# Four more norms in columns, five convolution taps and two product blocks moved to TensorE, and another order of row tiles

## Chip, cores and metric

The kernel runs on one core of one Trainium2 chip. The time is device microseconds of one execution, from the first instruction to the last with what lies around them; the lower the better. TensorE is called PE (its weight loads PEld), VectorE DVE, ScalarE ACT, GpSimd POOL, and SyncE SP, which here only issues transfers. SBUF is the memory on the core, and PSUM the eight banks (128 partitions of 512 fp32 numbers each) into which PE writes. A "wide" operation is one on 128x512 fp32.

## What is computed

Two transformer blocks on one sequence of 512 rows with 1024 channels, all in fp32. What the change touches, cut:

```python
def rmsnorm(x, g):
    y = x * rsqrt(mean(x * x, axis=-1, keepdims=True) + EPS)
    return y * g

def conformer_conv(hn, w_pw1, b_pw1, w_dw, b_dw, ln_g, ln_b, w_pw2, b_pw2):
    a, g = split(hn @ w_pw1 + b_pw1, 2)              # 1024 -> 2 x 1024
    u = a * sigmoid(g)
    u = causal_depthwise_conv(u, w_dw, width=31) + b_dw
    u = silu(layernorm(u, ln_g, ln_b))
    return u @ w_pw2 + b_pw2

# first block, layer 0: convolution; layer 1: 16 heads of forgetting attention
h = h + conformer_conv(rmsnorm(h, mix_norm[0]), ...)
h = h + square(relu(rmsnorm(h, ffn_norm) @ w1)) @ w2
h = h + sigmoid(rmsnorm(h, ple_norm) @ w_gate) * (p @ w_proj)
...
x = rmsnorm(h, final_norm)
# second block
hn = rms_norm(x, mix_norm_gain)
# hn @ w_in gives a linear recurrence, 8 heads of block attention and
# qx for 4 heads of 128 that attend to a memory of 256 rows
mk, mv = split(rms_norm(mem, mem_norm_gain) @ w_mem_kv)
p = softmax(qx @ mk.T * 128 ** -0.5); y_c = p @ mv    # per head
x = x + (sum of gated branches) @ w_out
x = x + (gelu(conv3(hn2 @ w_gate)) * (hn2 @ w_up)) @ w_down
return rms_norm(x, final_norm_gain)
```

## The kernel before

**Layout.** Activations lie transposed: a tile `h[:, k]` holds 128 channels of the 512 rows, and a 1024-wide tensor is eight tiles. A sum over channels is therefore a matmul with `inv_d`, a 128x128 matrix of 1/1024: squares of the eight tiles are added up by DVE in `acc_sq` (or by PE in PSUM), and one matmul with `inv_d` as the stationary operand gives the mean of squares in every partition, as a 128x512 row block. `norm` then adds EPS and takes the reciprocal on DVE (`var`), and ACT takes the root (`rstd`), all 512 wide. The other form stands in `col_stats`: four matmuls with one column of `inv_d` moving give the same mean as four columns of 128 rows, 128x4 in all.

**Products.** Each fp32 product is three matmuls in a faster fp32 form (`three`, L532 to L534): high times high, low times high, high times low. So each operand has a high and a low part. A block is 24 matmuls (8 channel tiles of the input, three each) into one bank, and it yields 128 output channels. Weights come from HBM in pieces of 1 MB, two parts of 128x1024 each. For every part ACT rounds the high half (L906, `next_w`), POOL subtracts it to get the low half (L435, `slab`), and PE's block waits for that. A ring of four parts lets the next one be made when a block of an older one has ended. The four banks `gp` take the products; the four banks `ms` take sums, scores and transposes.

**Order.** There is no scheduler: each engine runs its own program in the order in which it is written, and semaphores tie them. `next_w` and `slab` calls stand by hand between the other work of ACT and POOL.

**The stages, by the profile.** First norm and first product (to about 27 us); the convolution with the first product's other blocks (to 190); layer norm and second product (to about 250); feed-forward, gate, head attention, feed-forward, gate (to 1317); `qx`, memory attention (to 1362); gates, recurrence, block attention, feed-forward (to 2155); the last norm and the stores (to 2172).

**The convolution** goes over four pairs of channel tiles. Of the 31 taps of a tile, the first `POOL_TAPS[i]` are multiplied by ACT (`tap_products`) and added by POOL (`add_taps`, L458) in `pool_sum`; the others are one DVE step each (L1320), accumulating in a PSUM bank `ms`. `Weave` alternates the two tiles of a pair. `whole` adds the two sums. In between PE does the rest of the first product, two projections of p (`project`), the memory's statistics (`memory_stat`, `memory_turn`), and the products for memory keys and values (`memkv`), which need the memory's low half `m_lo` from POOL; then `mean` adds up the eight conv tiles for the layer norm.

**Layer norm.** DVE subtracts the mean from eight tiles (L1317), ACT squares each (L1043), PE adds the squares up in a bank (L671) with one wide matmul each, DVE does EPS and the reciprocal, ACT the root; then for each tile DVE multiplies, ACT applies silu (L1049) and rounds, DVE makes the low half, and `pw2` starts.

**Memory attention** (`attention`) takes 16 steps, 4 heads by 4 row tiles: scores (L842), maximum on DVE, exponential on ACT, two transposes on PE (L720), a copy, two matmuls with the values (L733) giving rows by channels, the division by the sum on DVE in `o_sb`, and after each head four more transposes (`O_`), then rounding. The first products behind it start when its last low half is there.

**Head attention** (`head_attention`) works on pairs of heads by row tile `qb` = 0, 1, 2, 3, whose width is (qb + 1) x 128 since attention is causal; steps are `S_` scores, `T_` transposes, `V_` values. It runs for 8 pairs in the first block and 4 in the second.

**Tail.** After the last blocks DVE adds (`add_h`, L1317), ACT squares, DVE adds the squares, one wide matmul, EPS, reciprocal, root, then eight wide DVE products into `h` and four stores.

## Time and profile before

| | |
|---|---|
| time, median of 3 runs | 2174.54 us (2173.0 to 2176.71) |
| profiled execution's own time | 2173.63 us |
| its span, first to last instruction | 2171.6 us |
| mean granted TensorE clock | 0.987 of full speed |
| PE, PEld busy | 2095.2 us, 1708.5 us |
| DVE, ACT, POOL busy | 1025.3, 799.8, 937.9 us |
| data read from HBM | 197.73 MB, 94 GB/s over the span |

The page gives for each engine its busy time as a share of the span, then for groups of instructions the mean length of one and the idle time just ahead of them with the instruction that ended it. The timeline gives single instructions or short runs of the same instruction, with the start in microseconds from the beginning of the span; a bracket at the end says how long the engine had been idle and on what it had waited. An fp32 matmul that isn't in the faster form shows as two records of one line. Matmuls are pipelined, so that one of 512 columns is listed with 0.39 us although the next starts 0.23 us after it.

### The profile page before, as it was taken

The page shows a single profiled execution, that of the slowest core. Times are in us where ns is not written, and L with a number is a line of the kernel's source. Part 1 is how long each engine was busy: PE and PEld are TensorE (multiplying, and loading weights), DVE is VectorE, ACT ScalarE, POOL GpSimd, SP SyncE. Part 2 cuts the span into 40 slices and gives each one's busy share as a digit, 9 for nine tenths or more (in the row PEclk, how much of TensorE's full clock was granted, in tenths as well). Part 3 has the DMA queues.
Part 4 walks back from the last instruction along what each step waited for, and adds up shares of the span by engine and source line. Part 5 has one row for each costly group of instructions (what it writes and reads, how often), then busy time and mean ns, then how long its engine had stood idle before and what let it go on. Part 6 is the DMA issues. An engine that isn't in the chain of part 4 may idle for free.

```text
span 2171.6 us, 26817 instructions
## 1 busy us (share of the span) xinstructions
PE 2095.2 (96%) x10024; PEld 1708.5 (79%) x10024; DVE 1025.3 (47%) x1584; ACT 799.8 (37%) x1213; POOL 937.9 (43%) x435
## 2 busy tenths in 40 slices
PE   7977999999999999999999998999999999999997
PEld 6765888888888876888888887778967888888885
DVE  7996432132355547442231356463354456254463
ACT  6645422222343248332222355252245343232231
POOL 5875454444444420354444442434442444444441
PEclk9988999999999999999999999999999999999998
DMA  4331242222222221332222221222211222322221
GB/s 189 112 131 59 80 154 97 97 97 97 97 97 99 98 78 41 116 117 97 97 97 97 97 88 49 83 97 97 89 67 53 84 97 97 104 90 103 91 97 58
DMA packets 32201, 205.28 MB, mean 95 GB/s; under 512 B 4448, under 2 KB 4576, under 8 KB 9072
## 3 DMA queue, kind: packets, MB, share of 16 engines
q1 hardware_dynamic: 31824, 199.87, 26.1%
q10 hardware_dynamic: 288, 4.19, 0.5%
q8 instruction: 59, 0.97, 0.2%
q14 instruction: 30, 0.25, 0.0%
HBM read 197.73 MB, written 6.32 MB: 94 GB/s over the span
## 4 chain that ended last, share of the span: by engine, by line
PE 58%; issue 24%; POOL 11%; DVE 5%; ACT 2%; DMA 0%; POOLq 0%; DVEq 0%; ACTq 0%
PE gp L532 18%; PE gp L533 18%; PE gp L534 18%; POOL w_lo L435 9%; DVE ms L1320 2%; POOL pool_sum L458 1%; DVE var L1346 0%; PE ms L671 0%; ACT w_hi L906 0%; PE ms L611 0%; DVE T L1317 0%; ACT T L1171 0%; PE ms L842 0%; DVE acc_sq L1317 0%; PE gp L808 0%
## 5 line engine op out<-in xcount | busy, mean ns | idle before, releaser
L435 POOL TENSOR_TENSOR w_lo<-raw,w_hi 128x1024 fp32r<-128x1024 f32 x350 | 847.6, 2424 | 1141.6 <-ACT w_hi L906 1124.1
L532 PE MATMUL gp<-a_hi,w_hi 128*128 128x512 f32 x1440 | 564.9, 392 | 12.4 <-DVE a_lo L1320 9.9
L906 ACT ACTIVATE w_hi<-raw 128x1024 fp32r<-128x1024 f32 x349 | 365.9, 1051 | 530.4 <-PE gp L534 525.6
L533 PE MATMUL gp<-a_lo,w_hi 128*128 128x512 f32 x1440 | 561.0, 390 | 0.0
L534 PE MATMUL gp<-a_hi,w_lo 128*128 128x512 f32 x1440 | 561.0, 390 | 0.0
L532 PE MATMUL gp<-b_hi,w_hi 128*128 128x512 f32 x1184 | 464.1, 392 | 8.6 <-DVE b_lo L1317 8.6
L533 PE MATMUL gp<-b_lo,w_hi 128*128 128x512 f32 (+1 forms) x1216 | 471.6, 388 | 0.0
L534 PE MATMUL gp<-b_hi,w_lo 128*128 128x512 f32 x1184 | 461.6, 390 | 0.0
L532 PEld LDWEIGHTS gp<-a_hi,w_hi 128*128 128x128 f32 x1440 | 271.0, 188 | 71.8 <-issue 13.1
L533 PEld LDWEIGHTS gp<-a_lo,w_hi 128*128 128x128 f32 x1440 | 271.1, 188 | 57.2 <-issue 1.5
L534 PEld LDWEIGHTS gp<-a_hi,w_lo 128*128 128x128 f32 x1440 | 270.7, 188 | 56.5
L1317 DVE TENSOR_TENSOR h<-gp,h 128x512 f32<-128x512 f32 x104 | 71.8, 692 | 429.9 <-PE gp L534 429.9
L532 PEld LDWEIGHTS gp<-b_hi,w_hi 128*128 128x128 f32 x1184 | 222.9, 188 | 56.9 <-issue 10.1
L533 PEld LDWEIGHTS gp<-b_lo,w_hi 128*128 128x128 f32 x1216 | 230.1, 189 | 47.3 <-issue 1.2
L534 PEld LDWEIGHTS gp<-b_hi,w_lo 128*128 128x128 f32 x1184 | 222.8, 188 | 46.4
L1317 DVE TENSOR_TENSOR T<-gp,rstd 128x512 f32<-128x512 f32 x136 | 93.8, 690 | 311.7 <-PE gp L534 308.7
L1320 DVE SCALAR_TENSOR_TENSOR ms<-u_pad,par,ms 128x512 f32<-128x512 f32 x178 | 120.5, 746 | 0.6
L915 ACT ACTIVATE sqb<-h 128x512 f32<-128x512 f32 x63 | 39.7, 632 | 146.7 <-DVE h L1317 127.4
L1320 DVE SCALAR_TENSOR_TENSOR T<-gpad,par,T 128x512 f32<-128x512 f32 x48 | 83.4, 1737 | 5.2 <-DVE T L1891 0.2
L458 POOL TENSOR_TENSOR pool_sum<-pool_sum,sqb 128x512 f32<-128x512 f32 x54 | 68.6, 1287 | 14.1 <-ACT sqb L975 13.9
L1064 ACT ACTIVATE b_hi<-U 128x512 fp32r<-128x512 f32 x32 | 20.3, 633 | 121.3 <-DVE U L1320 121.3
L1064 ACT ACTIVATE a_hi<-U 128x512 fp32r<-128x512 f32 x32 | 20.3, 633 | 120.4 <-DVE U L1320 120.4
(289 smaller groups left out, 1906.4 us busy)
## 6 DMA issues: line engine op xcount, KB each, us to landing
raw<-w_hbm SPq DMA_DIRECT2D x176, 1024.0 KB, 4.9
proj_scratch<-kT ACTq DMA_DIRECT2D x2, 2048.0 KB, 6.6
fbias<-negc_scratch SPq DMA_DIRECT2D x16, 256.0 KB, 3.4
h<-x_hbm SPq DMA_DIRECT2D x4, 512.0 KB, 7.1
u_pad<-proj_scratch SPq DMA_DIRECT2D x1, 2048.0 KB, 9.7
big<-proj_scratch SPq DMA_DIRECT2D x1, 2048.0 KB, 8.7
out_hbm<-h SPq DMA_DIRECT2D x4, 512.0 KB, 2.7
mem_raw<-mem_hbm SPq DMA_DIRECT2D x1, 1024.0 KB, 12.1
```

What stands on the lines that cost most here:

```text
L435: g.tensor_tensor(at(w_lo), src, f32(at(w_hi)), ALU.subtract).then_inc(w_lo_done, 1)
L458: g.tensor_tensor(pool_sum[:, s], pool_sum[:, s], sqb[:, s], ALU.add).then_inc(pool_conv, 1)
L532: pe.matmul(o, wh, xh, start=start, stop=False)
L533: pe.matmul(o, wh, xl, start=False, stop=False)
L534: return pe.matmul(o, wl, xh, start=False, stop=stop)
L906: act.activation(at(w_hi), src, ACT.Copy).then_inc(w_hi_done, 1)
L915: act.activation(dst, h[:, c], ACT.Square).then_inc(sq_done, 1)
L1064: act.activation(H_[0][:, k], U[:, k % 2], ACT.Copy).then_inc(hi_done, 1)
L1317: return v.tensor_tensor(o, a, b, op)
L1320: return v.scalar_tensor_tensor(o, a, s, b, op0, op1)
```

## The change

**1. Norms in columns.** For the first norm, the layer norm, the norm ahead of the second block (two chained norms, `gate[1]` and `fin`) and the last one, the wide mean, EPS, reciprocal and root are replaced. `columns` gives the mean as 128x4 in PSUM, `inverse_column` (DVE) does EPS and reciprocal on 128x4, `root_of` (ACT) the root. `diagonal` puts each of the four columns on the diagonal of a 128x128 matrix (two on DVE, two on ACT), and `spread` multiplies them with `inv_d`, which fills a bank with the root as rows in every partition. DVE copies it to `rstd`, or reads it in the bank. In the first norm the columns are made inside the first product, which now takes two blocks side by side (`first_blocks`, hook at the eighth channel tile).

**2. Convolution.** Pair 3 has five taps on POOL instead of eight, five on PE (`pe_taps`: a matmul of the shifted tile with the tap's weights on a diagonal, made by ACT in `diagonals`) and 21 on DVE instead of 23. PE's taps come first in the bank; DVE waits for them (`pe_tap_done`) and adds to them. PE's taps stand between the first and second half of the second projection, which is split likewise on ACT. The memory turn and the means use bank `ms[0]`, and the turn now waits for the end of the third pair's first sum. On POOL the weight part 23 moves from ahead of `m_lo` to behind it. One of four value tiles (of `memkv`) moves behind the layer norm's `spread`.

**3. Weight parts at the layer norm.** On ACT the part 28 is rounded after the last square, 29 after the first silu, 30 after the last silu and the two last value copies.

**4. Memory attention.** The values are stationary, so that a step's output comes with channels on partitions and the four turning transposes and `o_sb` go; probabilities are divided by their sum before they are transposed (`weighted`). Two blocks of the next product (`gxg`) stand inside: behind the second scores, and behind the last.

**5. Row tiles.** Both head attentions take the row tiles in the order 0, 3, 1, 2.

**6. Tail.** The last tile's squares go to the columns without DVE's addition. ACT and POOL scale tiles 0 and 1, DVE the other six; five stores in another order.

```diff
-POOL_TAPS = (9, 7, 7, 8)
+POOL_TAPS = (9, 7, 7, 5)
+PE_TAPS = (0, 0, 0, 5)
...
-STAT_TAP, COLUMN_TAP, KEYS_TAP = 3, 2, 15
+STAT_TAP, COLUMN_TAP, KEYS_TAP = 3, 4, 13
...
+ROW_TILE = (0, 3, 1, 2)
...
+
+        def pe_diag(s, n):
+
+            return T[:, 2 * s, n * P:n * P + P] if n < 4 else U[:, 1, s * P:s * P + P]
...
-            slab(Pos(23))
             g.wait_ge(m_hi, 1)
             g.tensor_tensor(M[1], mem_raw[:], f32(M[0]), ALU.subtract).then_inc(m_lo, 1)
-            add_taps(3, {3: [24], 5: [25], 7: [26], 9: [27], 12: [28], 13: [29]})
-            slabs(pw2["slab"] + 2, gq["slab"] + AHEAD)
+            add_taps(3, {1: [23], 3: [24], 4: [25], 5: [26], 7: [27]})
...
+            g.wait_ge(rows_copied, 1)
+            for k in range(2):
+                g.wait_ge(out_scaled, k + 1)
+                g.tensor_tensor(h[:, k], h[:, k], rstd[:], ALU.mult).then_inc(out_first, 1)
```

PE:

```diff
+            def columns(src, at, start=True, stop=True):
+
+                for t in range(QB):
+                    m = pe.matmul(at[:, t:t + 1], src[:, t * P:t * P + P], inv_d[:, 0:1], start=start, stop=stop, skip_group_check=True)
+                return m
...
+            def spread(n, diag, bank):
+
+                pe.wait_ge(diag_v, 2 * n + 2)
+                pe.wait_ge(diag_a, 2 * n + 2)
+                for t in range(QB):
+                    m = pe.matmul(bank[:, t * P:t * P + P], inv_d[:], diag[:, t * P:t * P + P], start=True, stop=True,
+                                  skip_group_check=True)
+                m.then_inc(row_done, 1)
+
+            def x_columns():
+                pe.wait_ge(acc_done, x0["acc"] + 7)
+                columns(acc_sq, ms[:, 1]).then_inc(stat_x, 1)
...
+            def pe_taps(s):
+                pe.wait_ge(u_done, 7 + s)
+                pe.wait_ge(diag_done, PE_TAPS[3] * (s + 1))
+                for n in range(PE_TAPS[3]):
+                    m = pe.matmul(ms[:, 1 + s, :], pe_diag(s, n), u_of(6 + s, TAPS - PE_TAPS[3] + n), start=(n == 0),
+                                  stop=(n == PE_TAPS[3] - 1))
+                m.then_inc(pe_tap_done, 1)
+            first_blocks(pw1[0], A, x0["split"], hook=x_columns, hook_k=7)
+            spread(0, x_diag, ms[:, 3])
+            pair(0, 2)
...
-            project(0)
+            project(0, 0)
+            project(0, 1)
             pair(3)
-            project(1)
+            project(1, 0)
+            pe_taps(0)
+            pe_taps(1)
+            project(1, 1)
             memory_turn()
...
-            for s in range(2):
-                slab_xs(Pos(memkv["slab"] + 4 + 2 * s), Pos(memkv["blk"] + 4 + 2 * s), M, 2)
...
+            slab_xs(Pos(memkv["slab"] + 4), Pos(memkv["blk"] + 4), M, 2)
+            slab_xs(Pos(memkv["slab"] + 6), Pos(memkv["blk"] + 6), M, 1)
             mean(6)
             mean(7).then_inc(mean_done, 1)
             for k in range(8):
                 pe.wait_ge(csq_done, k + 1)
-                pe.matmul(ms[:, 2, :], inv_d[:], sqb[:, k % 2], start=(k == 0), stop=(k == 7)).then_inc(cvar_done, 1)
+                if k == 0:
+                    clear_columns(ms[:, 3])
+                columns(sqb[:, k % 2], ms[:, 3], False, k == 7).then_inc(cvar_done, 1)
+            spread(1, ln_diag, ms[:, 1])
+            slab_xs(Pos(memkv["slab"] + 6), Pos(memkv["blk"] + 6), M, 1, 1)
             first_blocks(pw2, B, ln["split"])
...
+                def T_(i):
+                    pe.wait_ge(weighted, at["weighted"] + i + 1)
...
+                    for kb in range(2):
+                        m = pe.matmul(gp[:, 2 + j % 2, t * P:t * P + P], mv[:, kb, j * P:j * P + P],
+                                      probT[i % 4][:, kb * P:kb * P + P], start=(kb == 0), stop=(kb == 1), skip_group_check=True)
+                    m.then_inc(pv_done, 1)
+
+                for i in range(N + 4):
+                    if i < N:
+                        S_(i)
+                    if i in (1, N):
+                        slab_ws(Pos(gxg["slab"] + i // N), Pos(gxg["blk"] + i // N), A)
+                    if 3 <= i < N + 3:
+                        T_(i - 3)
+                    if i >= 4:
+                        V_(i - 4)
+            memory_attention()
...
-            gemm(gxg, A)
+            for c in range(2):
+                pe.wait_ge(lo_done, xat["split"] + 3 + c)
+                rest_of(gxg, A, 2 + c, 3 + c)
+            rest_of(gxg, A, 4, 8)
...
+            pe.wait_ge(acc_done, f["acc"] + 6)
+            columns(acc_sq, ms[:, 1], False, False)
+            pe.wait_ge(sq_done, f["sq"] + 8)
+            columns(sqb[:, 1], ms[:, 1], False, True).then_inc(stat_x, 1)
+            spread(4, end_diag, ms[:, 0])
+            spread(4, end_diag, ms[:, 2])
```

ACT and DVE (`columns`, `diagonal` and the attention steps that only follow the same pattern are left out):

```diff
-                         {5: lambda: sigmoid(3, 0), 10: lambda: sigmoid(3, 1), 12: lambda: projected(1, 0)})
-            projected(1, 1)
-            next_w(Pos(23 - AHEAD))
-            tap_products(3, {4: [24], 6: [25], 8: [26], 10: [27], 13: [28], 14: [29]}, {})
-            for s in range(2):
-                memory_values(s)
-            next_of(memkv, 7)
+                         {1: lambda: diagonals(0), 3: lambda: diagonals(1), 5: lambda: sigmoid(3, 0), 10: lambda: sigmoid(3, 1),
+                          12: lambda: projected(1, 0, 4)})
+            tap_products(3, {4: [23], 5: [24], 6: [25], 7: [26], 9: [27]}, {1: lambda: projected(1, 4, 5), 3: lambda: projected(1, 5, 8)})
...
                     act.wait_ge(cvar_done, k - 1)
...
+            next_w(Pos(28 - AHEAD))
+            act.wait_ge(c_inv, 2)
+            root_of(1, colv[:])
+            diagonal(1, ln_diag)
             for k in range(8):
                 act.wait_ge(normed, k + 1)
                 if k >= 2:
@@ -1049,6 +1115,10 @@
                 act.activation(U[:, k % 2], big[:, k], ACT.Silu, bias=col("ln_b", k), scale=col("ln_g", k)).then_inc(silu_done, 1)
...
                 act.activation(b_hi[:, k], U[:, k % 2], ACT.Copy).then_inc(hi_done, 1)
+                if k == 0:
+                    next_w(Pos(29 - AHEAD))
+            memory_values(1)
...
 
@@ -1128,51 +1198,18 @@
...
+                def H_(j):
+                    act.wait_ge(pv_done, at["pv"] + 4 * (j + 1))
+                    act.activation(b_hi[:, 4 + j], gp[:, 2 + j % 2], ACT.Copy).then_inc(hi_done, 1)
...
+            def inverse_column(n, src):
+
+                v.tensor_scalar(colv[:], src, EPS, 2.0 ** -20, ALU.add, ALU.mult).then_inc(c_eps, 1)
+                v.wait_ge(c_eps, n + 1)
+                v.reciprocal(colv[:], colv[:]).then_inc(c_inv, 1)
+
+            def diagonal(n, diag):
+
+                v.wait_ge(root_done, n + 1)
+                for t in range(2):
+                    v.tensor_scalar(diag[:, t * P:t * P + P], ident[:], root[:, n % 2, t:t + 1], None, ALU.mult).then_inc(diag_v, 1)
+            v.wait_ge(stat_x, 1)
...
+                src, sum_ = u_of(c, t), conv_bank(i, s)
+                if n == 0 and i == 3:
+                    v.wait_ge(pe_tap_done, s + 1)
...
+            inverse_column(1, ms[:, 3, 0:QB])
+            diagonal(1, ln_diag)
+            v.wait_ge(row_done, 2)
             for k in range(9):
                 if k < 8:
...
+            v.wait_ge(row_done, 5)
+            for k in range(2, 8):
+                stt(h[:, k], h[:, k], col("final2", k), ms[:, 0], ALU.mult, ALU.mult).then_inc(out_ready, 1)
```

**Where instructions stand.** PE at the end of the second projection, in a row before: `p_hi`, `p_lo` are the projection, `inv_d,U` is the memory turn, `b_lo` the first product on the memory.

```order
L532 MATMUL gp<-p_hi,w_hi 128x512
L533 MATMUL gp<-p_lo,w_hi 128x512
L534 MATMUL gp<-p_hi,w_lo 128x512
L634 MATMUL ms<-inv_d,U 128x1 [waits u_done,mrstd_done]
L634 MATMUL ms<-inv_d,U 128x1
L532 MATMUL gp<-b_lo,w_hi 128x256 [waits evacuated0,w_lo_done,mem_lo]
```

And now:

```order
L555 MATMUL gp<-p_hi,w_hi 128x512
L556 MATMUL gp<-p_lo,w_hi 128x512
L557 MATMUL gp<-p_hi,w_lo 128x512
L695 MATMUL ms<-u_pad,T 128x512 [waits tap_diagonal,u_done]
L695 MATMUL ms<-u_pad,T 128x512 x3
L695 MATMUL ms<-u_pad,U 128x512
L695 MATMUL ms<-u_pad,T 128x512 [waits tap_diagonal,u_done]
L695 MATMUL ms<-u_pad,T 128x512 x3
L695 MATMUL ms<-u_pad,U 128x512
L555 MATMUL gp<-p_hi,w_hi 128x512 [waits evacuated0,w_lo_done,p_lo_done]
```

The ten taps stand ahead of the projection's second half, and the turn comes behind that half.

ACT at the layer norm before (`sqb<-u_pad` are the squares, `rstd` the root, `U` the silu, `b_hi` its rounding):

```order
L1043 ACTIVATE sqb<-u_pad 128x512 [waits centred,proj_stored1]
L1043 ACTIVATE sqb<-u_pad 128x512 [waits centred]
L1043 ACTIVATE sqb<-u_pad 128x512 [waits cvar_done,centred] x6
L925 ACT_TABLE_LOAD
L925 ACTIVATE rstd<-var 128x512 [waits var_done]
L1049 ACT_TABLE_LOAD
L1049 ACTIVATE U<-u_pad,par 128x512 [waits normed]
L1051 ACTIVATE b_hi<-U 128x512 [waits silu_done]
```

And now:

```order
L1106 ACTIVATE sqb<-u_pad 128x512 [waits centred,proj_stored1]
L1106 ACTIVATE sqb<-u_pad 128x512 [waits centred]
L1106 ACTIVATE sqb<-u_pad 128x512 [waits cvar_done,centred] x6
L955 ACTIVATE w_hi<-raw 128x1024 [waits blk_done,raw_ready0]
L1001 ACT_TABLE_LOAD
L1001 ACTIVATE root<-colv 128x4 [waits column_inv]
L998 ACTIVATE T<-ident,root 128x128 [waits root]
L998 ACTIVATE T<-ident,root 128x128
L1115 ACT_TABLE_LOAD
L1115 ACTIVATE U<-u_pad,par 128x512 [waits normed]
L1117 ACTIVATE b_hi<-U 128x512 [waits silu_done]
L955 ACTIVATE w_hi<-raw 128x1024 [waits blk_done,raw_ready0]
```

A weight part comes between the last square and the root, and another behind the first silu; the root is four columns wide.

PE at the start of memory attention before (`mkv,qx` are scores, `ident,T` transposes, `mkv,U` values):

```order
L842 MATMUL ms<-mkv,qx 128x256 [waits evacuated2,evacuated3,evacuated1,evacuated0]
L842 MATMUL ms<-mkv,qx 128x256 [waits exped] x2
L720 MATMUL ms<-ident,T 128x128 [waits exped]
L720 MATMUL ms<-ident,T 128x128
L842 MATMUL ms<-mkv,qx 128x256 [waits exped]
L720 MATMUL ms<-ident,T 128x128 [waits exped]
L720 MATMUL ms<-ident,T 128x128
L733 MATMUL gp<-mkv,U 128x128 [waits pt_copied]
L733 MATMUL gp<-mkv,U 128x128
L842 MATMUL ms<-mkv,qx 128x256 [waits exped]
```

And now, first the start, then what follows the block of 24:

```order
L683 MATMUL ms<-T,inv_d 128x128 [waits diag_act,diag_dve]
L683 MATMUL ms<-T,inv_d 128x128 x3
L852 MATMUL ms<-mkv,qx 128x256 [waits evacuated0]
L852 MATMUL ms<-mkv,qx 128x256
L555 MATMUL gp<-a_hi,w_hi 128x512 [waits evacuated0,w_lo_done]
```

```order
L852 MATMUL ms<-mkv,qx 128x256 [waits exped] x2
L859 MATMUL ms<-ident,T 128x128 [waits weighted]
L859 MATMUL ms<-ident,T 128x128
L852 MATMUL ms<-mkv,qx 128x256 [waits exped,evacuated1]
L859 MATMUL ms<-ident,T 128x128 [waits weighted]
L859 MATMUL ms<-ident,T 128x128
L870 MATMUL gp<-U,mkv 128x128 [waits pt_copied,evacuated2]
L870 MATMUL gp<-U,mkv 128x128
```

A whole block stands behind the second scores, the transposes wait for weighted probabilities, and the values are now the stationary operand (`gp<-U,mkv`).

## Rows read from the trace of the kernel before

**Rows 1.** Page, part 1: busy us (share of span) xinstructions, by engine.

```profile
PE 2095.2 (96%) x10024; PEld 1708.5 (79%) x10024; DVE 1025.3 (47%) x1584; ACT 799.8 (37%) x1213; POOL 937.9 (43%) x435
```

**Rows 2.** Timeline, tail: start us, length us, engine, line, operation [idle before <-releaser].

```profile
2149.61 0.69 DVE L1317 TENSOR_TENSOR h<-gp,h 128x512 f32<-128x512 f32 x1 [4.15 <-PE gp L534]
...
2155.05 0.69 DVE L1317 TENSOR_TENSOR h<-gp,h 128x512 f32<-128x512 f32 x1 [4.15 <-PE gp L534]
...
2163.12 5.39 DVE L1320 SCALAR_TENSOR_TENSOR h<-h,par,rstd 128x512 f32<-128x512 f32 x8 [0.70 <-ACT rstd L925]
```

**Rows 3.** Timeline of the start, PE and DVE.

```profile
19.80 2.07 PE L611 MATMUL ms<-acc_sq,inv_d 128*128 128x512 f32 x2 [2.75 <-DVE acc_sq L1317]
...
29.54 0.75 DVE L1320 SCALAR_TENSOR_TENSOR u_pad<-ms,par,T 128x512 f32<-128x512 f32 x1 [0.79 <-ACT T L960]
```

**Rows 4.** Timeline of the convolution, DVE, with one row of PE.

```profile
96.11 11.94 DVE L1320 SCALAR_TENSOR_TENSOR ms<-u_pad,par,ms 128x512 f32<-128x512 f32 x18
...
145.66 1.39 DVE L1408 TENSOR_SCALAR ms<-u_pad,par 128x512 f32<-128x512 f32 x2
...
155.04 0.58 PE L532 MATMUL gp<-b_lo,w_hi 128*128 128x256 f32 x1 [8.84 <-POOL b_lo L476]
...
187.68 0.69 DVE L1317 TENSOR_TENSOR u_pad<-ms,pool_sum 128x512 f32<-128x512 f32 x1 [2.90 <-POOL pool_sum L458]
189.59 4.87 DVE L1317 TENSOR_TENSOR u_pad<-u_pad,ms 128x512 f32<-128x512 f32 x8 [1.22 <-PE ms L661]
```

**Rows 5.** Timeline of the layer norm and the product behind it.

```profile
200.90 3.35 DVE L1346 RECIPROCAL var<-var 128x512 f32<-128x512 f32 x1
...
204.94 1.28 ACT L1049 ACT_TABLE_LOAD   x1
...
206.23 0.81 ACT L1049 ACTIVATE U<-u_pad,par 128x512 f32<-128x512 f32 x1
...
208.69 0.77 PE L532 MATMUL gp<-b_hi,w_hi 128*128 128x512 f32 x1 [8.55 <-DVE b_lo L1317]
...
222.34 0.39 PE L532 MATMUL gp<-b_hi,w_hi 128*128 128x512 f32 x1
```

**Rows 6.** Timeline of memory attention and the sums before it, PE.

```profile
1317.34 1.02 PE L830 MATMUL ms<-acc_fin,inv_d 128*128 128x512 f32 x2
1318.20 0.95 PE L833 MATMUL ms<-inv_d,acc_sq 128*128 128x1 f32 x8
1319.01 1.03 PE L833 MATMUL ms<-inv_d,acc_fin 128*128 128x1 f32 x8
...
1331.43 1.10 PE L842 MATMUL ms<-mkv,qx 128*128 128x256 f32 x4 [1.73 <-DVE qx L1320]
...
1343.18 0.60 PE L842 MATMUL ms<-mkv,qx 128*128 128x256 f32 x2
...
1344.28 0.60 PE L842 MATMUL ms<-mkv,qx 128*128 128x256 f32 x2
...
1349.46 0.60 PE L842 MATMUL ms<-mkv,qx 128*128 128x256 f32 x2
...
1361.87 0.49 PE L532 MATMUL gp<-a_hi,w_hi 128*128 128x512 f32 x1 [1.69 <-DVE b_lo L1317]
```

**Rows 7.** Head attention: busy us in one period; timeline of a widest tile.

```profile
829.40:838.70 9.30, 9.11 (x88) 5.68 (x86) 7.11 (x30) 7.76 (x26) 0.00 (x0) 1.00 0.17 56
...
859.16 0.69 DVE L1676 CUSTOM_DVE_ANT_0 T<-gp,fbias 128x512 f32<-128x512 f32 x1 [1.41 <-PE ms L797]
```

**Rows 8.** Page, part 5: groups, busy us, mean ns | idle before, releaser.

```profile
L435 POOL TENSOR_TENSOR w_lo<-raw,w_hi 128x1024 fp32r<-128x1024 f32 x350 | 847.6, 2424 | 1141.6 <-ACT w_hi L906 1124.1
...
L906 ACT ACTIVATE w_hi<-raw 128x1024 fp32r<-128x1024 f32 x349 | 365.9, 1051 | 530.4 <-PE gp L534 525.6
...
L458 POOL TENSOR_TENSOR pool_sum<-pool_sum,sqb 128x512 f32<-128x512 f32 x54 | 68.6, 1287 | 14.1 <-ACT sqb L975 13.9
```

**Rows 9.** Waits of PE, whole span: us in total, times, longest us.

```profile
PE ms L797 <- DVE T L1687: 3.9, 5, 1.1
```

448 lines of the change are left out of this document (211 added, 237 removed).

## The prediction

> **What bounds the kernel now.** I read the busy line of the page first: the tensor engine (PE) is busy 96% of the span, the next engine half of it [rows 1]. So the time is PE's program plus its gaps, and a change pays where it takes products away from PE or closes a gap in which PE waits. Next comes PE's timeline, for every place where two products start further apart than their length. From about 223 us on one block of a 1024x1024 product (24 matmuls) ends every 5.44 us, as the two additions at the end show (2149.61 and 2155.05) [rows 2]; vector engine (DVE), scalar engine (ACT) and GpSimd (POOL) only have to keep up. Five places are left. (1) The first norm: PE waits 2.75 us up to 19.80 for the sum of squares [rows 3]. (2) The convolution: PE waits 8.84 us up to 155.04, while DVE works tap by tap [rows 4]. (3) The layer norm behind it: 8.55 us of waiting up to 208.69 [rows 5]. (4) Memory attention, 1331.43 to 1361.87, with small products and waits [rows 6]. (5) The tail, from the last addition at 2155.05 [rows 2] to the end of the span, 2171.6. The two head attentions are nearly full: in one period of four row tiles PE is busy 9.11 of 9.30 us [rows 7].
>
> **Prices.** A full fp32 matmul of 512 columns holds PE 0.85 us (1317.34 to 1318.20); four column matmuls take 0.81 (1318.20 to the next group, 1319.01) [rows 6]. So a norm in columns gives PE nothing; it shortens DVE's part, where one reciprocal over 128x512 takes 3.35 us [rows 5]. Spreading the root back is four matmuls of 128 columns, together one of 512: 0.85. A tap costs DVE 11.94/18 = 0.66 us [rows 4], PE 0.85, and on POOL 1.29 for the addition. A weight part costs ACT 1.05 and POOL 2.42 [rows 8]. Diagonal making is nowhere in the trace: 128x128 on DVE or ACT lies between 0.2 (the 4-wide steps, with their hand-over) and 0.4 (half of a 128x256 step); I take 0.3.
>
> **The start.** The first two blocks now run side by side: 42 matmuls before the statistic instead of 24, so the sum of squares (there before 19.80) no longer holds PE. Columns, two 4-wide DVE steps, a 4-wide root, the diagonals, a spread and a copy give DVE the row at about 24.9 instead of 26.7, and block 2 of the pair is there at once: the first gated input, at 29.54 now [rows 3], comes at about 27. PE is 4 us ahead, but DVE is the longer chain, so 2.5 us count.
>
> **The convolution.** Pairs 0 to 2 are unchanged and DVE has no gap in them, so pair 3 begins at 145.66 - 2.5 = 143.2 [rows 4]. It has 42 taps on DVE instead of 46: 27.8, with the memory column and keys 1.6 and the two sums 1.3, done at 173.9. Today it is ready too, but POOL is not: DVE waits 2.90 us at 187.68 for POOL's sum, after another wait before it [rows 4]. POOL loses six of its 14 additions (7.7 us) and the weight part ahead of the memory's low half: that half (2048 columns, so a little under twice a part's 2.42: 4.5 us) is done at about 146, then five parts and eight additions, 22.4, with some 2 of waiting: 170.6, hidden. PE gets ten taps, 8.5 us, right behind the first half of the second projection at about 133.5, where it waits now. With the second half of the projection (5.4) and about 1.4 for products at 1.2 GHz it reaches the memory's products at 149, finds the low half ready (the 8.84 us go), and needs 11.5 + 5.1 + 8.7 + 1.7 for memory keys, six means, three value tiles and the last two means: 176.3. DVE's first centring, at 189.59 now, comes then: 13.3 earlier, and PE is late by 2 us over DVE. The two are nearly even.
>
> **The layer norm.** The squares and their sums stay paced by a PE step per tile (0.81 for 0.85): 10.3 us, to 186.7. Now 200.90 + 3.35 is a reciprocal, and the root follows it. In the change DVE has its 4-wide result at 187.2, but ACT comes from the last square (185.5) through a weight part (1.05) and the table load (1.28 [rows 5]) and takes the root at 187.8. Diagonals, spread and product: 190.4. PE fills the gap with the fourth value tile (2.9). But new waits arise: weight part 29 is rounded only after the first silu, so POOL has its low part at 190.4 + 0.81 + 0.63 + 1.05 + 2.42 = 195.4 (0.81 is the silu [rows 5]; 0.63, the rounding behind it, I put between that and half of a part's 1.05), and part 30 only after all eight silus at 1.42 each: ACT is there at 204.7, POOL at 207.2. The third block of this product starts at 222.34 now [rows 5], so **15.1 us are gained** here, though the norm alone looks like more. Between 208.69 and 222.34 PE did 48 matmuls in 13.65 us, where 10.9 are needed at 2.4 GHz; that this loss at 1.2 GHz goes or stays changes nothing, since part 30 is later anyway. Ends: 10 (PE's tiles behind DVE at 1.2 GHz, 3 to 5 us) and 18 (POOL and ACT without any waiting).
>
> The trace has the silu start at 206.23, right behind the load that began at 204.94 and took 1.28 [rows 5]. The Trainium skill (ScalarE: Activation LUTs, "What ACT_TABLE_LOAD costs") adds a drain of about 1.38 us to each switch of table, 2.66 in all. With it the root would come 1.4 us later here and at the tail, and the sum would be 2.8 us worse, 2141.6. The trace shows no such drain, so the row decides.
>
> **Memory attention.** The sums before it cost PE the same as today: two 0.85 matmuls go, two 0.85 spreads come. DVE's two long reciprocals go, so the queries are there as PE ends their blocks, and scores start at 1329.4 instead of 1331.43. A step of scores, transposes and values is 1.10 us (1343.18 to 1344.28); with the turning of each head's output and its waits four steps take 6.28 now (1343.18 to 1349.46) [rows 6]. The turning goes. 16 steps at 1.10 and two product blocks at 5.44 are 28.5; the first block covers the first softmax. I add 2.0, because ACT has about 1.15 per step. The third block starts at 1359.9, against 1361.87 + 10.88 = 1372.75: **12.8 gained**. Ends: 7.3 (steps stay at 1.57) and 14.8. POOL's three clears before weight part 3 take 1 us and still end in time.
>
> **The tail.** After 2155.05: addition 0.7, square 0.65, columns 0.85, two steps 0.45, root 0.25 (its table load, 1.28 long, starts with the square's end and is just over), diagonals 0.6, spread 0.9, six products at 0.67: 2163.6. The other two tiles go over ACT and POOL (0.85 + 0.65 + 2 x 1.29 from 2159.5) and also end at 2163.6. Today the products end at 2163.12 + 5.39 and the span 3.1 us later [rows 2], so the end lies at 2166.7 to 2168: **4.4 gained**, 3 to 5.
>
> **The row tiles.** The order 0, 3, 1, 2 gives each step of PE a more even load. There is little to win: 0.19 idle in 9.30, twelve such periods, and the ends of both stages; PE waits 3.9 us in all for DVE's weighted rows [rows 9]. **2.5 gained**, from 8 gained to 2 lost.
>
> The sum is 15.1 + 12.8 + 4.4 + 2.5 = 34.8 off the profiled execution's 2173.6: 2138.8. The median shown, 2174.5, lies 0.9 above, so I say **2139**.
>
> **Rivals.**
> - The convolution gains less: PE's taps at 1.2 GHz (1.7 instead of 0.85 each) hold up the projection, ACT waits there in front of its products for POOL, and all comes 6 us later. For it: PE slows after each of today's waits; against: nothing waits ahead of the taps. 2145.
> - Memory attention keeps today's pace, and the second block hides nothing: 7 of the 12.8 stay. For it: ACT has as much to do per step as PE. 2146.
> - Everything hides and the row order takes up the small gaps between instructions: 5 from it, 3 more from the convolution. 2131.
> - The new row order starves PE: the widest tile comes second, and its two maxima (0.69 each [rows 7]), its two exponentials, about as long each, and the weighting, 3.7 us, stand open in each of 12 periods: 44 us, and 2185, slower than now. It decides from 3.1 us a period. Against it: between the wide tile's scores and its transposes PE has about 6 us of other tiles.
>
> **Chances.** Forecast (2134 to 2142) 0.58, convolution weak 0.16, attention weak 0.10, everything hides 0.12, starved 0.04. About 0.2% is what a measurement can tell here. The range holds all but the last and the edges of the others: 2130 to 2149. All but the starved case are faster: 0.95, and 0.02 within 0.2%, 0.03 slower.
>
> **What would show it.** Right: the first centring near 176; the third block of the product behind the layer norm at 207, with PE waiting for POOL's low weight part; the third block behind memory attention 12 to 13 us closer to the query blocks; a tail of 12 us after the last addition; head attention periods of 9.1 to 9.3. Wrong: a wait of DVE for PE's taps at the start of pair 3, a gap between POOL's additions beyond 174, or waits of PE for weighted rows in every period. The forecast would fail by the place of ACT's weight parts above all, as several of them wait in front of work on the path.

## The result, and the profile after

| | before | changed |
|---|---|---|
| median | 2173.77 us (4 runs, 2172.93 to 2176.71) | 2150.98 us (4 runs, 2148.33 to 2151.75) |
| span of the profiled execution | 2171.6 | 2148.5 |
| granted clock, mean | 0.987 | 0.991 |

The ratio of the runs is 0.9888, 95% interval 0.9875 to 0.9900; the medians lie 22.8 us apart (0.9895). I had forecast 34.8 us, and 2139 with a range to 2149: the direction was right, the gain half again as large as what came, and the time lies 2 us above the range. The changed kernel timed once more later gave 2150.36 (0.9878, 0.9859 to 0.9898).

The busy line of the page, against [rows 1]:

```profile
PE 2103.2 (98%) x10144; PEld 1723.6 (80%) x10144; DVE 1010.2 (47%) x1584; ACT 802.7 (37%) x1230; POOL 932.8 (43%) x432
```

PE has 8 us more work and DVE 15 us less; the idle part of PE shrank from 76.4 to 45.3 us. Laid side by side, the two traces give the gain stage by stage, each by the time at which the same instruction begins:

| stage | from, to | before | changed | gain | predicted |
|---|---|---|---|---|---|
| start, convolution, layer norm | 0 to the third block behind it | 222.34 | 212.45 | 9.9 | 15.1 |
| first head attention | first scores to the product behind | 788.91 to 866.55 | 779.11 to 856.12 | 0.6 | } 2.5 |
| second head attention | last product to next product | 1609.51 to 1652.51 | 1588.14 to 1630.26 | 0.9 | } |
| memory attention with its norm | statistics to the third block | 1316.49 to 1372.89 | 1306.04 to 1351.43 | 11.0 | 12.8 |
| tail | last addition to the end | 2155.05 to 2171.6 | 2132.78 to 2148.5 | 0.8 | 4.4 |
| sum | | | | 23.2 | 34.8 |

(The spans differ by 23.1. The forecast had put the third block behind memory attention at 1372.75, two blocks of 5.44 behind 1361.87 of [rows 6]; in the trace of before it begins at 1372.89.) So two rows hold 8.8 of the 11.7 us that are missing: the first, nearly all of it in the layer norm, and the tail. In the second trace of the changed kernel, of an execution of 2152.99 us, the third block behind the layer norm comes at 215.66 and the first row would read 6.7. First the part that came out as forecast. Timeline of DVE and PE in the start and the convolution of the changed kernel (columns as in [rows 2]); it answers to [rows 3] and [rows 4]:

```profile
21.97 0.95 PE L671 MATMUL ms<-inv_d,acc_sq 128*128 128x1 f32 x8
...
25.75 0.69 DVE L1550 COPY rstd<-ms 128x512 f32<-128x512 f32 x1 [1.59 <-PE ms L683]
28.55 0.75 DVE L1393 SCALAR_TENSOR_TENSOR u_pad<-ms,par,T 128x512 f32<-128x512 f32 x1 [0.80 <-ACT T L1020]
...
135.14 3.59 PE L695 MATMUL ms<-u_pad,T 128*128 128x512 f32 x8
...
144.49 6.70 DVE L1393 SCALAR_TENSOR_TENSOR ms<-u_pad,par,ms 128x512 f32<-128x512 f32 x10
...
173.52 1.33 DVE L1390 TENSOR_TENSOR u_pad<-ms,pool_sum 128x512 f32<-128x512 f32 x2
176.97 1.28 DVE L1390 TENSOR_TENSOR u_pad<-u_pad,ms 128x512 f32<-128x512 f32 x2 [2.12 <-PE ms L719]
```

The first gated input comes at 28.55 (29.54 before), so the start gives 1.0 and not 2.5: the copy of the row runs from 25.75 to 26.44 and ends 1.5 later than I had it. Pair 3 runs from 144.49 to 174.85 without a gap. PE's five taps for the first tile end at 139.6, 4.9 us before DVE adds to them; those for the second end at 143.88, 1.3 us before DVE's step at 145.14. So DVE waits for neither, but the second margin is thin: at the low clock (1.7 us a tap instead of 0.85) it would be gone. The first centring comes at 176.97, where I had 176.3; before it came at 189.59. Up to here 12.6 of the forecast 13.3 us are there. POOL is no longer waited for.

Then the layer norm, ACT, DVE, POOL and PE, against [rows 5]:

```profile
178.68 10.63 PE L671 MATMUL ms<-inv_d,sqb 128*128 128x1 f32 x64
182.54 0.63 ACT L1106 ACTIVATE sqb<-u_pad 128x512 f32<-128x512 f32 x1 [0.26 <-PE ms L671]
184.29 0.63 ACT L1106 ACTIVATE sqb<-u_pad 128x512 f32<-128x512 f32 x1 [1.12 <-PE ms L671]
185.99 0.63 ACT L1106 ACTIVATE sqb<-u_pad 128x512 f32<-128x512 f32 x1 [1.07 <-PE ms L671]
...
189.35 0.16 DVE L1454 TENSOR_SCALAR colv<-ms 128x4 f32<-128x4 f32 x1 [7.50 <-PE ms L671]
...
189.76 0.21 ACT L1001 ACTIVATE root<-colv 128x4 f32<-128x4 f32 x1 [0.89 <-DVE colv L1456]
...
190.84 2.05 PE L683 MATMUL ms<-T,inv_d 128*128 128x128 f32 x8 [1.53 <-ACT T L998]
...
192.92 1.28 DVE L1390 TENSOR_TENSOR u_pad<-u_pad,ms 128x512 f32<-128x512 f32 x2 [2.44 <-PE ms L683]
...
193.65 0.82 ACT L1115 ACTIVATE U<-u_pad,par 128x512 f32<-128x512 f32 x1 [1.65 <-DVE u_pad L1390]
...
196.15 2.37 POOL L455 TENSOR_TENSOR w_lo<-raw,w_hi 128x1024 fp32r<-128x1024 f32 x1 [6.16 <-ACT w_hi L955]
...
197.19 1.88 DVE L1390 TENSOR_TENSOR b_lo<-U,b_hi 128x512 fp32r<-128x512 f32 x1 [2.98 <-PE gp L557]
...
199.35 0.75 PE L555 MATMUL gp<-b_hi,w_hi 128*128 128x512 f32 x1 [2.20 <-DVE b_lo L1390]
...
212.45 0.50 PE L555 MATMUL gp<-b_hi,w_hi 128*128 128x512 f32 x1 [0.34 <-POOL w_lo L455]
```

And the same stretch in windows (us from to; length, busy us and instructions of PE, PEld, DVE, ACT, POOL; the third number from the end is the granted clock):

```profile
178.70:182.00 3.30, 3.30 (x32) 3.30 (x31) 3.14 (x6) 1.84 (x4) 0.00 (x0) 1.00 0.00 0
182.00:189.30 7.30, 7.30 (x36) 7.22 (x36) 0.00 (x0) 4.40 (x6) 1.65 (x1) 0.52 0.00 0
189.30:192.90 3.60, 2.07 (x11) 2.09 (x11) 0.82 (x4) 2.19 (x4) 0.69 (x1) 0.50 0.00 0
192.90:199.30 6.40, 4.25 (x24) 4.04 (x23) 3.40 (x4) 3.74 (x5) 2.37 (x1) 0.76 0.00 0
```

The reader is to see four things. ACT's squares come 0.9 apart to 182.54 and then 1.7 apart, since each waits for a column group of PE. The granted clock in the same stretch falls from 1.00 to 0.52 and 0.50, that is from 2.4 to 1.2 GHz, while PE is busy 7.30 of 7.30 us. And DVE waits 2.98 us, up to 197.19, for PE: for the fourth value tile, whose input lies where DVE wants to write the first low half (2.1 us of it once the rounded half that it also needs is there, at 195.12). And this low half then takes 1.88 us, while POOL makes weight part 29 (196.15 to 198.52); before, with POOL idle, it took 0.69:

```profile
207.74 0.69 DVE L1317 TENSOR_TENSOR b_lo<-U,b_hi 128x512 fp32r<-128x512 f32 x1 [1.49 <-ACT b_hi L1051]
```

The third block waits for POOL's part 30 last, as I had said, for 0.34 us. But that part comes at 212.40 and not at 207.2, since ACT rounds it behind the silus, and they began late and were held up by DVE.

### The profile page after: what moved, and what is told of

It reads as the page before. It is cut to its first block, busy times and chain, and to the rows that moved or that the text cites. A ratio compares the mean times of both kernels' runs of the same rounds, so it can differ in the third digit from the quotient of the medians.

```text
span 2148.5 us, 27006 instructions
## 1 busy us (share of the span) xinstructions
PE 2103.2 (98%) x10144; PEld 1723.6 (80%) x10144; DVE 1010.2 (47%) x1584; ACT 802.7 (37%) x1230; POOL 932.8 (43%) x432
## 3 DMA queue, kind: packets, MB, share of 16 engines
q1 hardware_dynamic: 31968, 199.87, 26.4%
## 4 chain that ended last, share of the span: by engine, by line
issue 40%; PE 36%; POOL 18%; DVE 3%; ACT 1%; POOLq 0%; DMA 0%; DVEq 0%; ACTq 0%
POOL w_lo L455 16%; PE gp L555 12%; PE gp L557 11%; PE gp L556 11%; DVE ms L1393 2%; POOL pool_sum L478 1%; ACT sqb L1035 0%; PE gp L870 0%; PE gp L810 0%; DMA raw<-w_hbm 0%; PE gp L788 0%; ACT w_hi L955 0%; POOL b_lo L495 0%; POOLq L454 0%; PE ms L799 0%
## 5 line engine op out<-in xcount | busy, mean ns | idle before, releaser
L478 POOL TENSOR_TENSOR pool_sum<-pool_sum,sqb 128x512 f32<-128x512 f32 x48 | 61.2, 1288 | 12.8 <-ACT sqb L1035 12.7
```

The costliest lines, as they stand in the source:

```text
L478: g.tensor_tensor(pool_sum[:, s], pool_sum[:, s], sqb[:, s], ALU.add).then_inc(pool_conv, 1)
```

## Experiments

All are built on the changed kernel. In brackets behind a time stand the ratio to the kernel before, run beside it, and its 95% interval. The diffs are cut. In the tables "first product" is the first matmul of the second projection of the convolution, and "next stage" the first matmul of the feed-forward layer with a low part; between them PE does eight blocks. These come from one trace each and place a difference to 0.1 us; the times of whole runs of one kernel lie 1 to 5 us apart.

### e1: the value tile between the column groups

```diff
                 columns(sqb[:, k % 2], ms[:, 3], False, k == 7).then_inc(cvar_done, 1)
...
+                s, at = sp_.slot(RING, k // 4), k % 4 * 256
+                m = three(gp[:, vb, 0:256], M[0][:, k, P:2 * P], M[1][:, k, P:2 * P], w_hi[:, s, at:at + 256], w_lo[:, s, at:at + 256],
+                          k == 0, k == 7)
+            m.then_inc(blk_done, 1)
             spread(1, ln_diag, ms[:, 1])
-            slab_xs(Pos(memkv["slab"] + 6), Pos(memkv["blk"] + 6), M, 1, 1)
```

> The changed kernel, with the 24 matmuls of the fourth value tile set in threes behind each of the eight column groups of the layer norm instead of behind the spread. In the changed kernel the eight groups run from 178.68 to 189.3 with the granted clock at 1.00, then 0.55 and 0.50, the spread behind them at 0.50, the first low half waits 2.98 us for the value tile, and the third block starts at 212.45. Clock theory: half of the loss is that PE runs these small matmuls at 1.2 GHz. With more work between them it stays at 2.4: the groups take 9.6 us, the spread 0.85 instead of 1.7, the first product comes at about 194 instead of 199.35, and the third block at about 207, 5 us earlier. Rival, the clock costs nothing because squares set the pace: only the wait for the tile goes, the groups still take 10.6 or more, the third block comes at 209.5, 3 us earlier.

2152.11 us (0.9896, 0.9879 to 0.9912), not faster at all. The windows of this run (columns as above), from the first group on:

```profile
178.00:182.00 4.00, 4.00 (x36) 4.00 (x36) 3.19 (x6) 1.88 (x4) 0.00 (x0) 0.96 0.00 0
182.00:193.00 11.00, 11.00 (x54) 11.00 (x53) 0.00 (x0) 4.39 (x6) 2.35 (x1) 0.50 0.00 0
```

PE had waited 1.50 us ahead of the first group, as in all traces with eight groups, and had no gap in the 15 us behind it. The clock fell at 181.67 all the same and stayed at 0.50, and then each group with its three products took 2.35 us. Both expectations fail: three products of 256 columns between the groups don't keep the clock up, and the groups get dearer with them. The first product came at 199.92, the next stage at 247.79.

### e2: weight parts earlier

```diff
             memory_values(0)
+            next_w(Pos(28 - AHEAD))
+            next_w(Pos(29 - AHEAD))
...
-            next_w(Pos(28 - AHEAD))
             act.wait_ge(c_inv, 2)
...
-                if k == 0:
-                    next_w(Pos(29 - AHEAD))
+                if k == 1:
+                    next_w(Pos(30 - AHEAD))
             memory_values(1)
-            next_w(Pos(30 - AHEAD))
```

> The changed kernel, with ACT rounding weight parts 28 and 29 ahead of the squares, where it idles 4.90 us, and part 30 behind the second silu instead of behind the last. The prediction held that the third block is set by part 30: then it comes 3 us or more earlier than 212.45. Clock theory: PE reaches the third block only at 212.1 anyway, since its first product starts late, at 199.35; the gain is 0.5 us at most, and the root is not earlier either.

2148.21 us (0.9874, 0.9858 to 0.9890). In this trace PE never waits for POOL's part. First product at 200.82 and next stage at 246.06: 45.2 us, against 46.1 in both traces of the changed kernel. By the traces the parts are worth about 0.9 us and not 3. PE's wait for POOL's part at the third block was 0.3 us in the first trace of the changed kernel and 1.7 in the second, and 1.7 to 1.8 in e3, e4, e8 and e11, which share its code here (0.3 in e7), always behind a late first product; the median is 2.2 to 2.8 us below the two of the changed kernel, within the scatter of its runs. So the parts end last, but taking their wait away brings only 0.9: the two limits lie close together, and what made both late stands ahead of the first product.

### e3: row tiles in the old order

```diff
-ROW_TILE = (0, 3, 1, 2)
+ROW_TILE = (0, 1, 2, 3)
```

> The changed kernel with the row tiles of both head attentions in the order 0, 1, 2, 3 as before. The prediction gave the new order 2.5 us. The two traces show 0.6 us less from one product to the next over the first head attention and 0.9 over the second: then this run is 1.5 us slower than the changed kernel, and the first attention takes as long as before. Rival, the order does nothing and these 1.5 us come from drift elsewhere: no difference.

2152.21 us (0.9893, 0.9877 to 0.9910). Over the second head attention the next product starts 43.00 us after the last one, exactly as before the change, and 42.12 in the new order. The first takes 79.2 against 77.0. Its windows, in e3, then in the changed kernel, then before:

```profile
781.40:860.60 79.20, 75.46 (x674) 46.86 (x674) 57.88 (x232) 63.27 (x201) 2.35 (x1) 0.98 0.13 41
```
```profile
779.10:856.10 77.00, 73.46 (x674) 46.02 (x674) 58.12 (x232) 64.23 (x201) 2.36 (x1) 1.00 0.14 42
```
```profile
788.90:866.50 77.60, 73.95 (x674) 46.03 (x674) 57.83 (x232) 63.18 (x201) 2.36 (x1) 1.00 0.13 42
```

In e3 the clock had 0.98 here, since it was down from 790.39 to 793.80, which costs about 1.7 us; before the change the old order took 77.6. PE's waits in this stretch are the same 3.3 to 3.7 us in sum in all three. The new order is worth 0.6 + 0.9 = 1.5 us (forecast 2.5), and the starved case did not occur.

### e4: the two product blocks behind memory attention

```diff
                     if i < N:
                         S_(i)
-                    if i in (1, N):
-                        slab_ws(Pos(gxg["slab"] + i // N), Pos(gxg["blk"] + i // N), A)
...
+            rest_of(gxg, A, 0, 2)
             for c in range(2):
                 pe.wait_ge(lo_done, xat["split"] + 3 + c)
...
-                    if i in (9, 13):
-                        next_of(gxg, i // 4 - 2)
+                    if i == 9:
+                        next_of(gxg, 0)
                 H_(3)
             memory_attention()
+            next_of(gxg, 1)
```

> The changed kernel with the two product blocks of memory attention moved from inside it to behind it, and ACT's second weight part there with them. If the blocks cover the first softmax and the last weighting, they are worth what PE waits there: before the change about 2.6 us between the first scores and the first transposes and about 1.5 at the end, so 4 to 5.5 us slower than the changed kernel. If ACT sets the pace of the 16 steps, the blocks hide nothing: under 1 us.

2149.48 us (0.9883, 0.9866 to 0.9899). From the first scores to the third block: 1321.46 to 1354.32, 32.9 us, against 32.2 (1319.22 to 1351.43). So the blocks inside are worth 0.7 us, or a little more, since ACT's second weight part also left the steps here. The rows of e4 show what the first softmax costs without a block to cover it:

```profile
1321.46 1.03 PE L852 MATMUL ms<-mkv,qx 128*128 128x256 f32 x4
1323.34 1.16 PE L852 MATMUL ms<-mkv,qx 128*128 128x256 f32 x4 [0.85 <-ACT T L1255]
...
1325.24 0.67 PE L852 MATMUL ms<-mkv,qx 128*128 128x256 f32 x2 [0.53 <-ACT T L1255]
```

PE waits 0.85 and 0.53 us. In the kernel before it had waited 1.87 us for the first exponential. There the same stretch, first scores to third block, took 41.5 us (1331.43 to 1372.89). So with no block inside 8.6 of the 9.3 us are there: the gain of this stretch is the turning and the shorter chain, not the cover (up to 1.7 us of it is the clock, which before was down from 1333.94 to 1337.35).

### e8: ACT's weight parts at the product blocks

```diff
-                    if i in (9, 13):
-                        next_of(gxg, i // 4 - 2)
+                    if i in (1, N):
+                        next_of(gxg, i // N)
```

> The changed kernel with ACT's two weight parts inside memory attention moved from the 9th and 13th step to the two places where PE runs a product block and ACT idles. In the changed kernel PE waits or slips 1.1 to 1.2 us behind each of the two parts. If these are the 1.9 us by which memory attention fell short of the prediction: 2 us faster from the first scores to the third block (32.2 us in the changed kernel). If the steps are bound elsewhere: no difference.

2147.67 us (0.9876, 0.9860 to 0.9893). First scores to third block: 1322.45 to 1354.21, 31.8 us, 0.4 less (this trace is of an execution of 2152.36 us; the other three took 2147.5 to 2147.7). In the changed kernel most steps start 1.10 us apart, but the values of two steps come 2.26 behind the ones before them. In e8 they come 1.79 behind, and 0.77 us of waiting for ACT's copy came in the last group. So the parts are a quarter of the missing 1.8 us, and the two slips stay, with 0.69 each. They stand where a head ends, in the changed kernel (first slip) at:

```profile
1334.06 0.69 DVE L1390 TENSOR_TENSOR b_lo<-gp,b_hi 128x512 fp32r<-128x512 f32 x1 [0.70 <-ACT b_hi L1267]
...
1335.12 0.47 ACT L1256 ACTIVATE T<-ms,nmax 128x256 f32<-128x256 f32 x1 [0.82 <-DVE nmax L1812]
```

DVE waits for ACT's rounding of the head and makes its low half, and only then the next maximum, for which ACT waits. With 28.5 us for 16 steps and two blocks, as forecast, 3.7 us come on top, where I had added 2.0; PE stands idle in 2.0 of them.

### e5: wide matmuls behind each column group

```diff
                 columns(sqb[:, k % 2], ms[:, 3], False, k == 7).then_inc(cvar_done, 1)
+                fill(2, ms[:, 2])
```

(`fill(n, bank)` is n matmuls of 512 columns into that bank.)

> The changed kernel with two additional matmuls of 512 columns (0.23 us each, into a bank nobody reads) behind each of the eight column groups of the layer norm. In all traces with the column form the granted clock falls to 0.50 between 178.5 and 182 and stays there to 196, even in the run in which the value tile's products filled every gap between the groups. In the kernel before, with 512-column sums, the same stretch had 0.86. If what lowers the clock is the one-column matmuls and wide ones hold it: the clock stays at 1.00, the groups come 1.27 us apart (10.2 in all, against 10.7 to 13.3), the spread takes 0.85, the first product comes at about 196.5 instead of 199.9 to 202, and the run is 2 to 4 us faster. If the clock falls in this place whatever PE does: groups of 2.6 us, 10 us slower.

2157.65 us (0.9923, 0.9906 to 0.9939), 7 us slower than the changed kernel. The trace is of the fastest of its four executions, 2153.80 us.

```profile
177.00:180.00 3.00, 3.00 (x25) 2.83 (x24) 3.00 (x6) 1.39 (x3) 0.00 (x0) 1.00 0.00 0
180.00:194.20 14.20, 14.20 (x60) 13.23 (x58) 0.22 (x1) 4.92 (x7) 2.36 (x1) 0.50 0.00 0
```

The clock fell at about 180, earlier than in the changed kernel, and stayed down for the 14 us of the sums; the groups came 2.56 us apart. Two matmuls of 512 columns in each step did not hold it.

### e6 and e10: squares added by DVE, one column group

```diff
+            slab_xs(Pos(memkv["slab"] + 6), Pos(memkv["blk"] + 6), M, 1, 1)
             for k in range(8):
-                pe.wait_ge(csq_done, k + 1)
-                if k == 0:
-                    clear_columns(ms[:, 3])
-                columns(sqb[:, k % 2], ms[:, 3], False, k == 7).then_inc(cvar_done, 1)
-            spread(1, ln_diag, ms[:, 1])
-            slab_xs(Pos(memkv["slab"] + 6), Pos(memkv["blk"] + 6), M, 1, 1)
+            for _ in range(20):
+                pe.matmul(ms[:, 2], a_hi[:, 0, 0:P], a_hi[:, 1], start=True, stop=True, skip_group_check=True)
+            pe.wait_ge(cvar_done, 7)
+            columns(acc_sq, ms[:, 3]).then_inc(cvar_done, 1)
+            spread(1, ln_diag, ms[:, 1])
```

(This is e6; e10 leaves the 20 matmuls out. The diff shows PE's part; ACT squares the first tile into `acc_sq`, and on DVE an addition into it stands behind the centrings.)

> The changed kernel with the eight squares of the layer norm added up by DVE (7 additions of 0.68, as before the first product), one column group at the end instead of eight, the fourth value tile run by PE in the meantime, and 20 wide matmuls into an unread bank behind it. Clock theory: this takes the one-column work at the low clock off the path. Sum on DVE: 8 centrings of 0.61 and 7 additions, 10 us, done at 187.5; columns and root at 189, rows at 190.5, and the first low half waits for no value tile: first product at 193.5 to 195, third block at 206 to 208, 5 to 7 us faster than the changed kernel. If ACT's later parts set the third block after all, 3 us or less.

> As e6_dve_sums (squares added by DVE, one column group, value tile in the meantime), without the 20 additional matmuls. In e6_dve_sums the clock fell to 0.50 at about 186.5 all the same, as the one column group began, so the additional matmuls bought nothing: the same time as e6_dve_sums within 1 us. If they did hold the clock for a while: the spread and the group take the same 3.4 us, but the clock is down at 182, and it may be back earlier or later, 1 us either way.

e6: 2145.83 us (0.9867, 0.9851 to 0.9884). e10: 2146.69 us (0.9861, 0.9845 to 0.9878). The first product comes at 195.25 and 195.85, the next stage at 243.58 and 244.02. So taking seven of eight column groups off the path gives 4 to 5 us, and the 20 matmuls nothing that can be told: in e6 the clock was up to 186.49 and down when the one group ran, in e10 it was down from 183.24 on, while PE waited 6.70 us. The group takes 1.87 us and the spread 2.05 in both.

### e9: the layer norm in the wide form

```diff
-                if k == 0:
-                    clear_columns(ms[:, 3])
-                columns(sqb[:, k % 2], ms[:, 3], False, k == 7).then_inc(cvar_done, 1)
-            spread(1, ln_diag, ms[:, 1])
+                pe.matmul(ms[:, 3, :], inv_d[:], sqb[:, k % 2], start=(k == 0), stop=(k == 7)).then_inc(cvar_done, 1)
...
-            inverse_column(1, ms[:, 3, 0:QB])
-            diagonal(1, ln_diag)
-            v.wait_ge(row_done, 2)
+            v.tensor_scalar(var[:], ms[:, 3], EPS, None, ALU.add).then_inc(eps_done, 1)
+            finish_var(ln)
+            v.wait_ge(rstd_done, ln["norm"] + 1)
...
-                    tt(big[:, k], big[:, k], ms[:, 1], ALU.mult).then_inc(normed, 1)
+                    tt(big[:, k], big[:, k], rstd[:], ALU.mult).then_inc(normed, 1)
```

> The changed kernel with the layer norm alone put back to the wide form (eight sums of 512 columns, EPS and reciprocal on 128x512, root as rows), everything else as changed, the fourth value tile behind the sums. In the kernel before, the wide form took 13.9 us from the first square's sum (191.05) to the first normalised tile (204.95); in the changed kernel and its variants the column form took 14.5 (178.44 to 192.92) where the clock fell late and 17.1 (177.97 to 195.12) where it fell early. If the columns at 1.2 GHz eat what the short reciprocal saves, the wide form here takes 14 us again, PE has the value tile done in the meantime, the first product comes at about 195.5 and the third block at 208 to 209: 3 to 5 us faster than the changed kernel. If the columns pay for themselves as the prediction had it (5 us less on DVE): 2 us or more slower.

2146.08 us (2145.77 to 2147.02; 0.9861, 0.9844 to 0.9877). Its four runs lie below all eight of the changed kernel (2148.24 to 2152.99), and so do all 16 of the kernels without the eight groups (e6, e9, e10 and e12: 2142.89 to 2148.08); the intervals of the ratios of e9 and the changed kernel overlap. Timeline of PE, DVE and ACT, and the windows:

```profile
177.58 7.70 PE L730 MATMUL ms<-sqb,inv_d 128*128 128x512 f32 x16 [1.50 <-ACT sqb L1103]
...
186.04 3.35 DVE L1414 RECIPROCAL var<-var 128x512 f32<-128x512 f32 x1
...
190.08 1.28 ACT L1110 ACT_TABLE_LOAD   x1
190.09 1.29 DVE L1385 TENSOR_TENSOR u_pad<-u_pad,rstd 128x512 f32<-128x512 f32 x2 [0.69 <-ACT rstd L971]
191.37 0.81 ACT L1110 ACTIVATE U<-u_pad,par 128x512 f32<-128x512 f32 x1
...
193.90 0.77 PE L555 MATMUL gp<-b_hi,w_hi 128*128 128x512 f32 x1 [5.75 <-DVE b_lo L1385]
...
196.52 0.80 PE L555 MATMUL gp<-b_hi,w_hi 128*128 128x512 f32 x1 [1.00 <-POOL w_lo L455]
...
177.60:185.30 7.70, 7.70 (x18) 2.81 (x19) 3.39 (x6) 5.42 (x9) 0.17 (x1) 1.00 0.00 0
185.30:190.10 4.80, 2.85 (x24) 2.65 (x23) 4.05 (x3) 1.70 (x3) 2.23 (x1) 1.00 0.00 0
```

With sums of 512 columns the clock stays at 1.00 to beyond 190. They take 7.7 us for the eight tiles, the reciprocal that I had wanted to save takes its 3.35, and the first normalised tile still comes 12.5 us after the first sum, against 14.2 to 17.0 for the columns. The value tile (from 184.72) runs at full clock in PE's idle time behind the sums. PE's wait ahead of the first sum, 1.50 us, is the same as in the column kernels, so it isn't this wait alone that lowers the clock there. The kernel before says the same from the other side: there the clock was down already when the sums began, and came back while nothing but wide sums ran:

```profile
190.50:193.80 3.30, 2.75 (x4) 1.17 (x4) 3.30 (x7) 1.61 (x3) 1.71 (x1) 0.50 0.85 268
193.90:200.10 6.20, 6.20 (x14) 1.86 (x12) 0.56 (x1) 4.27 (x6) 0.00 (x0) 1.00 0.06 24
```

### e13: the value tile ahead of the means

```diff
-            slab_xs(Pos(memkv["slab"] + 6), Pos(memkv["blk"] + 6), M, 1)
+            slab_xs(Pos(memkv["slab"] + 6), Pos(memkv["blk"] + 6), M, 2)
...
             spread(1, ln_diag, ms[:, 1])
-            slab_xs(Pos(memkv["slab"] + 6), Pos(memkv["blk"] + 6), M, 1, 1)
```

> The changed kernel with the fourth value tile back ahead of the last two means, as before the change, and the columns kept. The tile costs PE 2.9 us at full clock, so the first square is 2.9 later; behind the spread the 4.6 us of the tile at the low clock and its hold on DVE's first low half go. If the form of the sums is what costs: the sums and rows take 14.5 to 17.1 us as before, the first product comes within 1.5 us of the changed kernel, and so does the time. If the tile's place was the loss: the first product 3 us or more earlier, and as fast as the wide form (2146).

> The changed kernel once more, for a comparison on one chip. In its first trace the clock fell at 182 and the product behind the layer norm began at 199.35; in five runs that share its code there the clock fell at 178.5 to 180 and that product began at 201.3 to 202.4. Expected: one of the two, 2148 to 2152 us.

e13: 2149.92 us (0.9884, 0.9865 to 0.9903), beside 2150.36 for the changed kernel on the same chip. The first product is earlier (197.76), but the next stage comes at 245.64, as in the first trace of the changed kernel (245.45): eight blocks took 47.9 us instead of 46.1, as they began at the low clock (to 204.39) and waited 0.78 us for POOL's part. In both traces the clock fell equally late, 3.6 us after the first sum. So the tile's place is worth nothing in the end; the form of the sums is what costs. All traces of this stage together:

| kernel | first sum | first normalised tile | first product | next stage |
|---|---|---|---|---|
| before | 191.05 | 204.95 | 208.69 | 255.21 |
| changed | 178.68 | 192.92 | 199.35 | 245.45 |
| changed, second time | 179.21 | 196.18 | 202.57 | 248.68 |
| e1 | 178.02 | 196.67 | 199.92 | 247.79 |
| e2 | 178.21 | 195.12 | 200.82 | 246.06 |
| e3, e4, e7, e11 | 178.09 to 178.65 | 195.19 to 195.33 | 201.58 to 201.71 | 247.72 to 247.80 |
| e8 | 179.33 | 196.26 | 202.66 | 248.72 |
| e5 | 177.05 | 197.81 | 204.21 | 250.33 |
| e13 | 180.28 | 194.51 | 197.76 | 245.64 |
| e6, e10 (one group) | 186.53, 187.13 | 192.00, 192.61 | 195.25, 195.85 | 243.58, 244.02 |
| e9, wide | 177.58 | 190.09 | 193.90 | 242.09 |
| e12, wide | 177.29 | 189.81 | 193.62 | 239.52 |

Seven of these traces have the changed kernel's code in this stage (changed twice, e3, e4, e7, e8, e11), and the first is the one in which it went best. In the 11 with eight column groups the clock fell 0.3 to 0.9 us after the first group began in seven, and 2.9 to 3.7 after it in the others (the first of the changed kernel, e1, e5, e13), and it came back only when products ran again.

### e7 and e11: the tail

```diff
# e7
             columns(acc_sq, ms[:, 1], False, False)
+
+            def fill(n):
+                for _ in range(n):
+                    pe.matmul(ms[:, 3, :], w_hi[:, 0, 0:P], a_hi[:, 0], start=True, stop=True, skip_group_check=True)
+            fill(2)
             pe.wait_ge(sq_done, f["sq"] + 8)
             columns(sqb[:, 1], ms[:, 1], False, True).then_inc(stat_x, 1)
+            fill(8)
# e11
-            for a, b in ((2, 4), (4, 6), (0, 2), (6, 7), (7, 8)):
+            for a, b in ((2, 4), (4, 6), (6, 7), (7, 8), (0, 2)):
```

> The changed kernel with 2 and 8 wide matmuls into an unread bank before and behind the last tile's column group, ahead of the two last spreads. In the changed kernel the granted clock is 0.50 there: the group takes 1.40, two spreads 3.75, DVE's products start 6.4 us behind the start of the last addition, and ACT's copy 8.1 behind it. Clock theory: at full clock the group takes 0.9, each spread 0.85, the products start at 5.1 and the copy at 5.9; POOL's two products end 2.2 us earlier, and the end comes 1.5 to 2 us earlier. Rival: the stores set the end, nothing or 0.5 us.

> The changed kernel with the store of tiles 0 and 1 (POOL's) issued last instead of third. In the changed kernel DVE's last tile is ready at 2143.24 and POOL's second at 2144.07, and the stores of DVE's last two tiles stand behind the wait for POOL. If that queue costs: 0.5 to 1 us earlier. If the 16 DMA engines are full to the end anyway (360 to 414 GB/s in that stretch): no difference.

e7: 2152.24 us (0.9891, 0.9874 to 0.9909). e11: 2151.35 us (0.9881, 0.9865 to 0.9898). Neither can be told from the changed kernel by its time. First the tail of the changed kernel, which answers to [rows 2]:

```profile
2132.78 0.69 DVE L1390 TENSOR_TENSOR h<-gp,h 128x512 f32<-128x512 f32 x1 [3.36 <-PE gp L557]
...
2134.19 1.40 PE L671 MATMUL ms<-inv_d,sqb 128*128 128x1 f32 x8 [0.44 <-ACT sqb L964]
...
2137.11 3.75 PE L683 MATMUL ms<-T,inv_d 128*128 128x128 f32 x16 [1.53 <-ACT T L998]
...
2139.20 4.04 DVE L1393 SCALAR_TENSOR_TENSOR h<-h,par,ms 128x512 f32<-128x512 f32 x6 [2.44 <-PE ms L683]
...
2140.91 0.60 ACT L1384 ACTIVATE rstd<-ms 128x512 f32<-128x512 f32 x1 [3.93 <-PE ms L683]
2141.58 2.49 POOL L536 TENSOR_TENSOR h<-h,rstd 128x512 f32<-128x512 f32 x2 [25.78 <-ACT rstd L1384]
...
2132.78:2135.60 2.82, 2.37 (x17) 2.20 (x16) 0.69 (x1) 1.91 (x2) 0.00 (x0) 0.85 0.00 0
2135.60:2139.20 3.60, 2.08 (x10) 2.12 (x11) 0.82 (x4) 0.91 (x3) 0.00 (x0) 0.50 0.00 0
```

The clock is at 0.50 when the two spreads run; they take 3.75 us, where two at full clock would be 1.7. DVE's products start 6.42 us behind the start of the last addition (8.07 before). They need the first spread alone; ACT's copy for POOL needs the second, and POOL's second product ends at 2144.07, 0.8 us behind DVE's last. From e7:

```profile
2137.29 3.42 PE L940 MATMUL ms<-a_hi,w_hi 128*128 128x512 f32 x8
...
2140.51 2.24 PE L683 MATMUL ms<-T,inv_d 128*128 128x128 f32 x16
...
2141.89 4.04 DVE L1399 SCALAR_TENSOR_TENSOR h<-h,par,ms 128x512 f32<-128x512 f32 x6 [3.29 <-PE ms L683]
```

The clock fell in spite of the additional matmuls; eight of them held PE to 2140.5, and the products start 6.92 behind. The tail is the same code in eleven other traces, and there the products start 5.15 (clock 0.99 in this stretch of e5) to 6.42 us (the changed kernel) behind the last addition, and the end comes 14.4 to 15.7 behind it. In every one of them the end lies 4.4 us behind the end of POOL's second product, so POOL's tiles and the stores behind them set the end, not DVE's. With POOL's store last this distance is 3.9 us in e11 and 4.3 in e12: 0.1 to 0.5 us, by the traces alone.

### e12: what helped, together

The wide layer norm (e9), the weight parts (e2), ACT's parts in memory attention (e8) and the order of stores (e11), with their diffs as above.

> The changed kernel with what helped put together: the layer norm in the wide form (e9), weight parts 28 and 29 rounded ahead of the squares and 30 behind the second silu (e2), ACT's parts inside memory attention at the product blocks (e8), POOL's store last (e11). In e9_ln_wide the third block waits for POOL's low part 30, made from 206.57 on (to about 209), while the two blocks before it are done at 206: with part 30 rounded at 195 this wait of 2.5 us goes. With 0.4 from memory attention and up to 0.5 from the store: about 3 us faster than e9_ln_wide, 2143, and 7 to 8 faster than the changed kernel. If part 30 was no wait there either, under 1 us faster than e9_ln_wide.

2143.57 us (2142.89 to 2144.33; 0.9854, 0.9836 to 0.9872), the fastest of all kernels here, 7 us below the changed one. PE waits for no weight part in this stretch, and the product's eight blocks take 45.9 us, where e9 had 48.2. The wait of 2.5 us for part 30 that the expectation names isn't in e9's trace: PE waits there for part 29 alone, 1.0 us (the row at 196.52), and for nothing from there to the next stage. So earlier parts are worth 1.0 of the 2.3 us. The other 1.3 go with the clock, which was down to 201.58 in e9 and to 197.78 in e12; that the parts brought it back earlier is not shown.

## Why the prediction was right or wrong

**Right.** What bounds the kernel, the sign, and the places. The convolution: first centring 12.6 us earlier (13.3 forecast), POOL hidden, PE's taps at full clock where nobody waits for them, so the rival with taps at 1.2 GHz fell (the clock was up again at 134.52, the taps began at 135.14). The pace of the steps in memory attention (1.10 us where nothing slips), and the scores' start (1319.22 + 10.45 us of earlier gain = 1329.67, forecast 1329.4). That the row order starves nobody. And no drain beside the table load, which the Trainium skill adds (ScalarE: Activation LUTs, "What ACT_TABLE_LOAD costs"): in e9 the load of 1.28 us began at 190.08 and the silu at 191.37, as in [rows 5], so the measurement decides.

**The layer norm, step by step (15.1 forecast, 9.9 measured).** The step that failed is "the squares and their sums stay paced by a PE step per tile (0.81 for 0.85)". I took 0.81 from four column matmuls that stand in the middle of full-clock products [rows 6], and carried it to a place where nothing else runs. There the clock falls in every one of the traces with the eight groups (between 178.4 and 184), and the group takes 1.70. The sums ended at 189.3 instead of 186.7, the spread took 1.7 instead of 0.85, and the value tile behind it 4.6 instead of 2.9. That part 30 comes last was right. But I had concluded from it that clock losses change nothing here, and this holds only for losses behind the first product: what comes ahead of it delays the silus too, and part 30 is rounded behind them. By the rows the first silu comes at 193.65 instead of 190.4, 3.2 us late, and with the silus held up behind it the part is there at 212.40 instead of 207.2. The second miss is the wait of DVE's first low half for the value tile, which I had counted as filling a gap of PE. e13 shows that taking it away alone brings nothing. A third I had not thought of: a low half takes 1.4 to 2.7 us instead of 0.7 while POOL makes a weight part (1.88 here). This meets the first, second or third low half in the trace of every kernel built on the changed one, the wide ones too, so it can't be the whole difference between them; no run removes it, and what it costs stays open.

What replaces the term: e9 against the changed kernel says that in this place the column form costs 3.4 to 6.6 us at the next stage (242.09 against 245.45 and 248.68; 1.1 to 1.6 of it lies ahead of the first sum already) and 4 to 5 us by the medians. The reciprocal of 3.35 that it saves is real. It is paid back, and more, with the eight groups.

**Start (2.5 forecast, 1.0 measured).** Same kind of error on a small scale: I had the row copied at 24.9 or so and it was complete at 26.4. The clock was up there; the chain of columns, steps, root, diagonals, spread and copy takes 4.5 us (21.97 to 26.44), 0.5 of it in hand-overs that I had not summed. By my prices it takes 3.7, so for 24.9 the columns would have had to begin at 21.2, and they began 0.8 later.

**Tail (4.4 forecast, 0.8 measured).** The term that was mis-sized is "spread 0.9" and with it the row. With hand-overs the row takes 5.15 us even at full clock, where I had 4.4, and 6.42 at the low one, where the spread takes 2.09. The second spread, for POOL's two tiles, takes 1.7 for the 0.85 that I had counted, so they end at 2144.07 and not with DVE. The end then lies 4.4 us behind them, at the far end of what I had allowed (3.1 to 4.4). Of the missing 3.6 us, 2.0 are the row, 0.8 POOL's tiles and 0.8 the stores; the clock is 1.3 of the row, and about 0.85 of POOL's.

**Memory attention (12.8 forecast, 11.0 measured).** A mis-sized term: 2.0 us added to the 28.5, 3.7 measured. Of these, two slips of 1.16 us come where a head ends, for its rounding and low half, which I had not counted, and for ACT's weight parts. The rival "the second block hides nothing" was right in what it says of the blocks (0.7 us), and wrong in that it took the gain from them.

**Row tiles (2.5 forecast, 1.5 measured),** within their range.

The range ended at 2149 since I had counted the weak cases one by one; here the column form fell short in the layer norm and in the tail at once, in both with the clock at 0.50, though in the tail the clock is about 2.1 of the 3.6 us that are missing.

What stays open: why the clock falls later in some executions (182.31 in the first trace of the changed kernel, 179.68 in the second), and what exactly makes it fall: in seven traces it fell so soon after PE's wait of 1.5 us that this wait may have its part in it. e1 and e5 show that it stays down for 11 and 14 us with PE busy without a gap, and e9 and the kernel before that it needn't in this place.

## What to carry to other kernels

Price a small operation at the clock of the place where it will run. The price read between dense products is not valid in a stretch where PE does only such small operations: there it was twice as high. Ask too what the other engines will be doing at that moment: here a step of DVE took two to four times as long beside POOL. A form that saves another engine's time but puts chains of tiny matmuls on PE must be weighed with that doubled price, and with what follows in the same stretch. And where a change has several sites for one idea, forecast them as one risk.

## What the runs showed of the hardware

- Column groups (four fp32 matmuls with one moving column) took 0.81 us at 2.4 GHz and 1.70 at 1.2; sums of the same length in 512-column form ran with the clock at 1.00 for 7.7 us in the same place (e9). In the kernel before the clock was at 0.50 when these sums began and back at 1.00 from 193.88 on, with nothing else running on PE.
- The clock fell and stayed at 0.50 with PE busy without a gap (e1: 15.0 of 15.0 us; e5: 17.2 of 17.2), so busy time as the profile counts it doesn't tell whether the clock will hold. Three matmuls of 256 columns (e1) or two of 512 (e5) behind each group didn't hold it.
- A step of DVE that reads both operands from SBUF takes longer while POOL makes a weight part: the low half 1.88 us for 0.69, and in the changed kernel's trace 25 steps `T<-gpad,par,T` of the second block have a median of 2.65 us beside POOL and 23 others 0.75. Steps with an operand in PSUM don't: `T<-gp,rstd` has a median of 0.69 in 78 such places and in 58 others.
- Extra matmuls meant to keep the clock up can arrive at the low clock themselves: eight took 3.2 us instead of 1.8, and delayed what they were to help.
- The same code took 14.4 to 15.7 us in the tail, 14.4 with the clock at 0.99 up to the products (e5) and 15.7 with 0.65 (the changed kernel). Runs of one kernel lie 1 to 5 us apart; that this comes from the clock too is likely, but was not shown.
- A table load of ACT takes 1.28 us, and the next step starts within 0.02 us of its end, if nothing else is missing ([rows 5], e9).
